# Moving the SBUF tensors of a two-layer decoder trunk to other start addresses modulo 512 bytes

## The reference

```python
for layer in range(DEPTH):                                   # 2
    x = x + 0.5 * swiglu(rmsnorm(x, norm_ffn1[layer]), w_ffn1_in[layer], w_ffn1_out[layer])
    h = rmsnorm(x, norm_mix[layer])
    x = x + (retention(h, ...) if layer % 2 == 0 else dsa_attention(h, ...))
    x = x + 0.5 * swiglu(rmsnorm(x, norm_ffn2[layer]), w_ffn2_in[layer], w_ffn2_out[layer])
return rmsnorm(x, final_norm)

def swiglu(h, w_in, w_out):                                  # 1024 -> 2 x 2816 -> 1024
    gate, up = jnp.split(h @ w_in, 2, axis=-1)
    return (jax.nn.silu(gate) * up) @ w_out
```

## Time and profile before

| what | before |
|---|---|
| median of 3 runs | 2121.27 us (2121.04 to 2121.82) |
| span of the profiled execution, first to last instruction | 2124.3 us |
| PE (matmul) busy | 2075.9 us, 98% of the span |
| PEld (weight load) busy | 1679.5 us, 79% |
| DVE / ACT / POOL busy | 960.4 (45%) / 592.6 (28%) / 245.0 us (12%) |
| chain that ended last | PE 94%, DVE 3%, ACT 1%, issue 1% |
| mean granted TensorE clock | 0.988 of full speed |
| DMA | 188.73 MB, mean 89 GB/s |

### The profile page before, as it was taken

One profiled execution on the slowest core, in us unless ns is written; L12 is line 12 of the kernel. 1 busy time (PEld: TensorE's weight loads), 2 busy tenths in 40 slices (PEclk: granted clock), 3 DMA queues, 4 the chain that ended last, 5 costly groups with the idle time before them and its releaser, 6 DMA issues.

```text
span 2124.3 us, 23288 instructions
## 1 busy us (share of the span) xinstructions
PE 2075.9 (98%) x9138; PEld 1679.5 (79%) x9138; DVE 960.4 (45%) x1173; ACT 592.6 (28%) x705; POOL 245.0 (12%) x155
## 2 busy tenths in 40 slices
PE   7999999999999999999999999999988899999997
PEld 5888888777877887888888788888866778888886
DVE  5444434433533444444434444443369754444322
ACT  4222222232222312222222222222155423222210
POOL 3000022111010231000022000002212050000121
PEclk9999999999999999999999999999989999999998
DMA  4222222222222222222223222222221022222221
GB/s 174 99 99 99 75 95 95 95 80 86 79 75 90 80 99 80 99 99 99 72 93 112 99 98 88 91 80 95 86 90 41 21 80 91 90 96 93 82 95 67
DMA packets 30962, 188.73 MB, mean 89 GB/s; under 512 B 3584, under 2 KB 3584, under 8 KB 14656
## 3 DMA queue, kind: packets, MB, share of 16 engines
q1 hardware_dynamic: 30672, 187.25, 25.3%
q0 software_dynamic: 240, 0.79, 0.1%
HBM read 185.92 MB, written 2.10 MB: 89 GB/s over the span
## 4 chain that ended last, share of the span: by engine, by line
PE 94%; DVE 3%; issue 1%; ACT 1%; DMA 0%; POOL 0%; POOLq 0%; DVEq 0%; SPq 0%; ACTq 0%
PE bank L1129 28%; PE bank L1130 28%; PE bank L1131 28%; PE bank L1135 2%; PE bank L1137 2%; PE bank L1136 2%; PE bank L1258 2%; DVE xn_lo L746 1%; PE bank L1248 1%; PE bank L1375 1%; PE bank L1364 1%; DVE w_lo L740 0%; PE bank L1412 0%; PE bank L1421 0%; DVE temp L1078 0%
## 5 line engine op out<-in xcount | busy, mean ns | idle before, releaser
L1129 PE MATMUL bank<-xn_hi,w_hi 128*128 128x512 f32 x1672 | 659.9, 395 | 17.2 <-DVE xn_lo L746 17.1
L1130 PE MATMUL bank<-xn_lo,w_hi 128*128 128x512 f32 x1672 | 653.5, 391 | 0.0
L1131 PE MATMUL bank<-xn_hi,w_lo 128*128 128x512 f32 x1672 | 653.0, 391 | 0.0
L478 ACT ACTIVATE w_hi<-w_raw 128x2048 fp32r<-128x2048 f32 (+2 forms) x195 | 335.7, 1721 | 1034.7 <-PE bank L1131 987.9
L740 DVE TENSOR_TENSOR w_lo<-w_raw,w_hi 128x2048 fp32r<-128x2048 f32 (+2 forms) x191 | 406.1, 2126 | 286.0 <-ACT w_hi L478 285.9
L1129 PEld LDWEIGHTS bank<-xn_hi,w_hi 128*128 128x128 f32 x1672 | 314.9, 188 | 89.8 <-DVE xn_lo L746 13.0
L1130 PEld LDWEIGHTS bank<-xn_lo,w_hi 128*128 128x128 f32 x1672 | 315.2, 189 | 67.0 <-issue 2.2
L1131 PEld LDWEIGHTS bank<-xn_hi,w_lo 128*128 128x128 f32 x1672 | 315.1, 188 | 66.9
L1129 PE MATMUL bank<-gated_hi,w_hi 128*128 128x512 f32 x704 | 279.1, 396 | 0.0
L1130 PE MATMUL bank<-gated_lo,w_hi 128*128 128x512 f32 x704 | 279.1, 396 | 0.0
L1131 PE MATMUL bank<-gated_hi,w_lo 128*128 128x512 f32 x704 | 279.1, 396 | 0.0
(11 more groups left out here) (154 smaller groups left out, 1597.6 us busy)
## 6 DMA issues: line engine op xcount, KB each, us to landing
w_raw<-w_ffn_in SPq DMA_DIRECT2D x87, 1024.0 KB, 4.8
w_raw<-w_ffn_out SPq DMA_DIRECT2D x64, 704.0 KB, 4.0
w_raw<-w_ret_in SPq DMA_DIRECT2D x24, 1024.0 KB, 4.8
w_raw<-w_ret_out SPq DMA_DIRECT2D x8, 1024.0 KB, 4.8
w_raw<-w_dsa SPq DMA_DIRECT2D x8, 1024.0 KB, 4.7
x_res<-x_in SPq DMA_DIRECT2D x4, 512.0 KB, 7.0
out<-x_res SPq DMA_DIRECT2D x8, 256.0 KB, 2.2
w_raw<-w_ffn_in SPq DMA_DIRECT2D x2, 512.0 KB, 6.8
```

The lines of the kernel that those rows point to most:

```text
L478: nc.scalar.activation(w_hi[u % 2][:, :size], w_raw[u % 2][:, :size], copy)\
L1129: mm(to, w_hi[slot][:, at:at + width], hi, start=start, stop=False)
L1130: mm(to, w_hi[slot][:, at:at + width], lo, start=False, stop=False)
L1131: return mm(to, w_lo[slot][:, at:at + width], hi, start=False, stop=stop)
```

## The change

The small tensors are placed first, ahead of the stream; 16512 + 248 (rounded to 256) + 64 + 32 + 32 = 16896, which is 0 modulo 512. Then 64 bytes are left free ahead of the weights and another 64 ahead of the arena. `head_r_col` goes to the arena, behind `decay`.

```diff
+LINE = 512
...
+    GAINS = 7 * CHUNKS + 6
+    gains = place("gains", GAINS)
+    minus_half = place("minus_half", 16)
+    mean_sq = place("mean_sq", BLOCKS)
+    r_col = place("r_col", BLOCKS)
+    assert top % LINE == 0
     x_res = place("x_res", CHUNKS * SEQ)
     xn_hi = place("xn_hi", CHUNKS * SEQ, FP32R)
     xn_lo = place("xn_lo", CHUNKS * SEQ, FP32R)
+    top += 64
     w_raw = [place(f"w_raw{n}", UNIT) for n in range(2)]
...
     diagonal = place("diagonal", SEQ)
-    GAINS = 7 * CHUNKS + 6
-    gains = place("gains", GAINS)
-    minus_half = place("minus_half", 16)
-    mean_sq = place("mean_sq", BLOCKS)
-    r_col = place("r_col", BLOCKS)
-    head_r_col = place("head_r_col", BLOCKS)
+    top += 64
     arena = top
...
     decay = place("decay", SEQ)
+    head_r_col = place("head_r_col", BLOCKS)
```

## The result

The changed kernel takes 2141.3 us (median of 4 runs, 2138.0 to 2142.8) against 2121.55 us for the kernel before in the same comparison: a ratio of 1.0087 (95% interval 1.0073 to 1.0101). It is slower by some 19 us (19.75 us between the medians). The forecast was 2099.6 us, faster. The value lies inside the stated range of 2050 to 2150, but with the wrong sign, and some 1 us from the 2140 us of the milder form of rival B: the arena gains, the stream loses.

What follows compares the result with a forecast made beforehand. PE, busy 98% of the span, was taken to bound the kernel by its matmuls' start-to-start interval. Arena -21.7 us, all else 0: 2121.3 - 21.7 = 2099.6 us (case A, chance 0.43), 8-in-10 range 2050 to 2150.

Steps and rivals of the forecast that it cites:

- rival B: Fp32r matmuls: operand distance counts and 0 is good; stream +41 us, 2162 us, or 2140 us if the arena gains; chance 0.24.
- What bounds the kernel: Whole kernel: PE is busy 98% of the span, so the matmuls' start-to-start interval changes the time one for one.
- That an address effect exists, and on which matmuls: Fp32r matmuls: 226.7 ns with the stream moving, 234.3 with the arena, an address effect of 7.6 ns a matmul.
- Rival D: Arena matmuls: the 7.6 ns come from something else that the change doesn't touch; 2121 us, chance 0.11.
- the odd 32 bytes: Arena operands: starting 32 bytes off a multiple of 64 was taken to cost 234.3 ns instead of 226.7.
- Stream from 128 to 0, weights from 128 to 64: The stream's 5400 matmuls: taken as 0, since operands stay at multiples of 64; bounds -58 to +41 us.
- Arena from 32 to 128: 2808 matmuls with the arena moving and 48 with latents stationary: 7.6 ns less each, -21.7 us.
- Plain float32, DVE, ACT, POOL, DMAs at 0: Float32 matmuls already at full rate, other engines hidden behind PE except at joints, weight loads under matmuls: 0.
- Its threshold of 230.7 ns: Stream's start-to-start interval above which the kernel gets slower even if the arena gains: a rise of 4.0 ns.
- Rival C: Fp32r matmuls: moving-tile and next-weight reads no longer meet; 2055 us half way to full rate, 2011 at full; chance 0.22.

## Why the prediction was wrong

- **What bounds the kernel**: right. All of the change is in the interval from start to start; PE's waits for the stream and the busy time of DVE, ACT and POOL stayed within 1 us.
- **That an address effect exists, and on which matmuls**: right, and it is what the whole change is. Rival D (nothing) is out.
- **"I take it that the odd 32 bytes is what costs, because it is the only property in which all the cheap groups agree"**: this is the step that failed. The cheap groups agreed in two properties, multiples of 64 and distance 0, as the text itself says under rival B. The run with all starts at 96 decides between them: 226.7 ns with nothing at a multiple of 64. Apart from the 24 matmuls of 72 columns, the rows of before held only distances 0, 160 and 96, and could not decide it.
- **"Stream from 128 to 0, weights from 128 to 64 ... I take 0"**: it follows from that step and cost most. In its place the 4992 matmuls of the stream rose by 6.7 ns, +33 us by the steady values and +29.7 us in the traces, since the matmuls behind each pause cost more already before, and the trace of before has more of them at the lower clock. The 384 by token rose by 6.7 ns, +2.5 us. The bound in the text, 234.3 ns and +41 us, held it.
- **"Arena from 32 to 128 ... -21.7 us"**: right in sign, but half as large again as what came. The arena went from distance 160 to 64, that is from 234.3 to 228.9 and not to 226.7: -14.4 us in the trace for `gated`, `ret` and `o`, and nothing for the latents (+0.2). Being worked out from the stream's value, it assumed a distance of 0 without saying so; with the arena at that distance the run measured 2100.8 us, 1.2 us from the forecast. So the number 2099.6 was a fair one for another change, the arena moved to the weights' own place and the stream left alone.
- **Plain float32, DVE, ACT, POOL, DMAs at 0**: right.
- **Rival B**: right in mechanism, with its milder form (+19 us, 2140) some 1 us from the result, partly since two errors cancel (234.3 in place of 233.3 for the stream, 226.7 in place of 228.9 for the arena). Its threshold of 230.7 ns was passed at 233.3. It was given 0.24. The 232 ns of rows 7 were evidence for it and were argued away by the length of the stretch. Rows 6 are no evidence either way: they are the stream's first intervals behind a pause, and in the trace it is at its steady 226.7 some 9 matmuls later. The 24 matmuls of rows 7 are longer than that, but they change their distance with every third one, so they never had one steady value.
- **Rival C**: out. No distance of the 64 tried goes below 226.7 ns with 512 columns.

## What to carry to other kernels

Where PE bounds a kernel with fp32r matmuls of 128 stationary and 512 moving columns, each with its own weight load, start both operands at the same place modulo 256 bytes, and at multiples of 32; here that is one line (`top += 96` ahead of the arena) and took 2123.7 to 2100.8 us. Look at the start-to-start interval of each group of matmuls, not at PE's busy share: two groups of equal shape with 389 and 396 ns in the profile are the sign. And when two properties divide the cheap rows from the dear ones in the same way, the forecast should carry both with near equal chances, or ask which of them the change keeps; this change kept the one and broke the other.

## What the runs showed that was not expected

- With both starts at multiples of 32 bytes, the interval of these matmuls depends on the distance of the two operands modulo 256 bytes, with PE alone at work: 226.7 ns at 0 and 234.2 at 160. In steps of 4 bytes the distance alone no longer sets it: two pairs at distance 240 gave 226.7 and 233.3 ns.
- The steady intervals at 0 (226.67 ns) and at most other distances (233.33) are 34 and 35 times 6.67 ns, and at +64 three intervals in a row (226, 229, 232) make 687, which is 103 times; at 160 seven intervals in a row (234, 231, 238, 237, 231, 234, 235) make 1640, which is 246 times. bf16's 215.8 is no multiple. With fp32r PE seems to fall in step with something of 16 cycles at 2.4 GHz; what it is wasn't looked into.
- The rule "same place" doesn't hold for 256 moving columns (120.0 ns at 0, 117.8 at 64) nor for 64 or 32 stationary ones (228.3 ns at 64 against 230.1 at 0, and 230.0 at 224 against 231.7 at 0).
- At one and the same distance, +64, two steady values were seen, 228.9 and 233.3 ns, in the kernel and with PE alone.
